# Block 2's pair entries: TensorE's product with the values issued ahead of the next entry's transposes, in one kernel of two transformer-like blocks

## The reference

```python
x = x + 0.5 * swiglu(rmsnorm(x, ffn1_norm[l]), ...)
h = rmsnorm(x, mix_norm[l])
(c_q, c_kv, k_rope, n_q, n_kc, n_vc, n_ks, n_vs, n_kw, n_vw, n_gate, sb_q, sb_k, sb_v) = jnp.split(h @ w_in[l], split_at, axis=-1)
o_mla = mla_attention(c_q, c_kv, k_rope, ...)          # 6 heads, causal
o_nsa = nsa_attention(n_q, n_kc, n_vc, n_ks, n_vs, n_kw, n_vw, gates, ...)   # 6 heads, three branches
o_sb = stick_breaking_attention(sb_q, sb_k, sb_v)      # 4 heads
x = x + concat([o_mla, o_nsa, o_sb]) @ w_out[l]
x = x + 0.5 * swiglu(rmsnorm(x, ffn2_norm[l]), ...)
```

```python
p = masked_softmax(q_block @ k.T * scale, mask)
o = p @ v
```

## Time and profile before

| | |
|---|---|
| Time, median of 3 runs | 3455.21 us (3454.33 to 3456.77) |
| Profiled execution | 3456.97 us, its span 3455.2 us |
| TensorE busy | 3352.7 us, 97% of the span |
| VectorE, ScalarE, GpSimd busy | 1668.8, 1223.1, 239.0 us |
| The two layers' stretches with pair entries | 1839.7 to 1999.0 us and 2904.0 to 3064.0 us |
| Granted TensorE clock over the execution | 0.991 of full speed |

### The profile page before, as it was taken

One profiled execution on the slowest core, in us unless ns is written; L12 is line 12 of the kernel. 1 busy time (PEld: TensorE's weight loads), 2 busy tenths in 40 slices (PEclk: granted clock), 3 DMA queues, 4 the chain that ended last, 5 costly groups with the idle time before them and its releaser, 6 DMA issues. The chain is left out here.

```text
span 3455.2 us, 42101 instructions
## 1 busy us (share of the span) xinstructions
PE 3352.7 (97%) x15684; PEld 2625.5 (76%) x15684; DVE 1668.8 (48%) x2158; ACT 1223.1 (35%) x1831; POOL 239.0 (7%) x268
## 2 busy tenths in 40 slices
PE   8999999999899999999999999999999999999998
PEld 6657888776688887888766688887888776678887
DVE  6755443566444335443545554435443554654433
ACT  4333122432422234232444442234223354542233
POOL 1200000011010000000102300002000101300000
PEclk9999999999999999999999999999999999999999
DMA  6213322321233232332321133333332321023332
GB/s 169 64 46 80 97 98 97 92 80 44 73 93 97 98 102 75 97 97 97 86 60 29 31 98 97 97 97 93 97 97 98 91 69 37 19 87 97 97 97 67
DMA packets 434262, 288.19 MB, mean 83 GB/s; under 512 B 44528, under 2 KB 412316, under 8 KB 433896
## 3 DMA queue, kind: packets, MB, share of 16 engines
q1 hardware_dynamic: 431272, 280.02, 27.9%
q0 software_dynamic: 2736, 4.58, 0.9%
q10 hardware_dynamic: 144, 2.10, 0.2%
HBM read 284.53 MB, written 2.13 MB: 83 GB/s over the span
## 5 line engine op out<-in xcount | busy, mean ns | idle before, releaser
L2018 PE MATMUL bank<-hh,whi 128*128 128x512 f32 x2768 | 1093.2, 395 | 20.3 <-DVE hl L1466 7.3
L2019 PE MATMUL bank<-hl,whi 128*128 128x512 f32 x2768 | 1079.7, 390 | 0.0
L2020 PE MATMUL bank<-hh,wlo 128*128 128x512 f32 x2768 | 1079.6, 390 | 0.0
L1400 DVE TENSOR_TENSOR wlo<-raw,whi 128x1024 fp32r<-128x1024 f32 (+2 forms) x534 | 646.4, 1212 | 309.4 <-ACT whi L944 295.0
L2018 PEld LDWEIGHTS bank<-hh,whi 128*128 128x128 f32 x2768 | 521.0, 188 | 154.9 <-issue 37.4
L944 ACT ACTIVATE whi<-raw 128x1024 fp32r<-128x1024 f32 (+2 forms) x534 | 546.4, 1034 | 258.3 <-PE bank L2020 257.8
L2020 PEld LDWEIGHTS bank<-hh,wlo 128*128 128x128 f32 x2768 | 520.8, 188 | 109.6
L2019 PEld LDWEIGHTS bank<-hl,whi 128*128 128x128 f32 x2768 | 521.1, 188 | 108.2 <-issue 2.6
L2018 PE MATMUL bank<-fshi,whi 128*128 128x512 f32 (+1 forms) x1358 | 525.6, 387 | 2.7 <-ACT G L1090 1.6
L2020 PE MATMUL bank<-fshi,wlo 128*128 128x512 f32 (+1 forms) x1358 | 521.8, 384 | 0.0
L2019 PE MATMUL bank<-fslo,whi 128*128 128x512 f32 (+1 forms) x1358 | 521.8, 384 | 0.0
(11 more groups left out here) (254 smaller groups left out, 2571.9 us busy)
## 6 DMA issues: line engine op xcount, KB each, us to landing
raw<-in_ffn_w_gate SPq DMA_DIRECT2D x88, 512.0 KB, 3.8
raw<-in_ffn_w_up SPq DMA_DIRECT2D x88, 512.0 KB, 3.8
raw<-in_ffn_w_down SPq DMA_DIRECT2D x88, 512.0 KB, 3.5
raw<-in_w_in SPq DMA_DIRECT2D x78, 512.0 KB, 3.9
raw<-in_w_up SPq DMA_DIRECT2D x64, 512.0 KB, 4.0
raw<-in_w_down SPq DMA_DIRECT2D x64, 512.0 KB, 3.4
raw<-in_w_out SPq DMA_DIRECT2D x16, 512.0 KB, 4.0
raw<-in_w_in SPq DMA_DIRECT2D x18, 256.0 KB, 3.3
```

The lines of the kernel that those rows point to most:

```text
L1400: dve.tensor_tensor(slot3(wlo, s, m), slot3(raw, s, m), slot3(whi, s, m).bitcast(F32), ALU.subtract).then_inc(c.lo_done.sem, 1)
L2018: pe.matmul(o, wh, ah, start=start, stop=False)
L2019: pe.matmul(o, wh, al, start=False, stop=False)
L2020: return pe.matmul(o, wl, ah, start=False, stop=stop)
```

## The change

In each step of `pair` TensorE now issues scores, then the product of entry j - 5, then the transposes of entry j - 4. No instruction is added or taken away, and the other engines' lists stay as they are. Lines shift in the changed kernel: the product is at L2167 (L2157 for `cmp`), the transposes at L2188 (L2183 for `cmp`).

```diff
--- before.py
+++ after.py
@@ -2142,26 +2142,6 @@
                     for head in range(2):
                         ins = pe.matmul(bank[:, sb_ + head, at:at + P], identb, causal, start=False, stop=True)
                     ins.then_inc(c.pair_qk.sem, 1)
-                k = j - T_LAG
-                if 0 <= k < n_entries:
-                    e = entries[k]
-                    if k:
-                        before = entries[k - 1]
-                        pt = c.pair_pt[before["act"]]
-                        pe.wait_ge(pt.sem, pt.at(l, before["moved"]))
-                    else:
-                        pe.wait_ge(c.cmp_sub.sem, c.cmp_sub.at(l, 1))
-                    if e["kind"] == "cmp":
-                        pe.wait_ge(c.cmp_p.sem, c.cmp_p.at(l, 1))
-                        for head in range(2):
-                            for i in range(QT):
-                                ins = pe.transpose(bank[0:32, 4 + head, P * i:P * i + P], g(C_P + 128 * (e["t"] + 3 * head) + 32 * i, 32), ident)
-                    else:
-                        pe.wait_ge(c.pair_scaled.sem, c.pair_scaled.at(l, 2 * e["q"] + 2))
-                        for head in range(2):
-                            for kt in range(e["i"] + 1):
-                                ins = pe.transpose(bank[:, 4 + head, P * kt:P * kt + P], p_tile(e, head, e["n"])[:, P * kt:P * kt + P], ident)
-                    ins.then_inc(c.pair_turned.sem, 1)
                 k = j - O_LAG
                 if 0 <= k < n_entries:
                     e = entries[k]
@@ -2187,6 +2167,26 @@
                                 ins = pe.matmul(bank[r[0]:r[1], 6, at:at + P], g(v, HD), pt_tile(e)[:, head, P * kt:P * kt + P],
                                                 start=e["first"] and kt == 0, stop=last and kt == e["i"])
                     ins.then_inc(c.pair_pv.sem, 1)
+                k = j - T_LAG
+                if 0 <= k < n_entries:
+                    e = entries[k]
+                    if k:
+                        before = entries[k - 1]
+                        pt = c.pair_pt[before["act"]]
+                        pe.wait_ge(pt.sem, pt.at(l, before["moved"]))
+                    else:
+                        pe.wait_ge(c.cmp_sub.sem, c.cmp_sub.at(l, 1))
+                    if e["kind"] == "cmp":
+                        pe.wait_ge(c.cmp_p.sem, c.cmp_p.at(l, 1))
+                        for head in range(2):
+                            for i in range(QT):
+                                ins = pe.transpose(bank[0:32, 4 + head, P * i:P * i + P], g(C_P + 128 * (e["t"] + 3 * head) + 32 * i, 32), ident)
+                    else:
+                        pe.wait_ge(c.pair_scaled.sem, c.pair_scaled.at(l, 2 * e["q"] + 2))
+                        for head in range(2):
+                            for kt in range(e["i"] + 1):
+                                ins = pe.transpose(bank[:, 4 + head, P * kt:P * kt + P], p_tile(e, head, e["n"])[:, P * kt:P * kt + P], ident)
+                    ins.then_inc(c.pair_turned.sem, 1)
 
             def compressed_scores(c, b, l):
```

## The result

The changed kernel took 3468.32 us in the median of six runs (3463.63 to 3474.04), the kernel before 3455.19 us in the six beside it (3453.40 to 3456.77). The ratio is 1.0037, with a 95% interval from 1.0027 to 1.0048: 13.1 us more, slower, and by more than the 0.2% that the prediction took as the least that can be told. The prediction was 3465.6 us in a range from 3458 to 3471, and slower. The profiled execution of the changed kernel took 3465.51 us (span 3463.7).

What follows compares the result with a forecast made beforehand. TensorE, busy 97% of the span, was taken as the bound. Delays of 4.85 us a layer, 9.7 for both, plus 0.8 for shape changes made 10.5; 3455.2 + 10.4 = 3465.6 us, range 3458 to 3471.

Steps and rivals of the forecast that it cites:

- main mechanism: Copies in pair steps have less cover; where slack is under the product's length, TensorE waits: 9.7 us for both layers.
- The reason for the sign: In pair steps VectorE's copy, not GpSimd's scaling, comes last and releases product and transposes together, so these waits gain nothing.
- First turn: From 1859.75 to the wait ending at 1874.42: late copies and late `hl` end that wait 1.05 us later a layer.
- VectorE is then busy without a break: After the late `hl`, VectorE has no idle time up to the copy awaited until 1874.42, so that wait ends 1.05 later.
- Behind `mix_lo`: In a turn's first step, transposes no longer run inside the wait for `hl` and add their length: 1.6 us a layer.
- ScalarE's copy: Transposes at 1934.70: the product in front makes ScalarE's copy end later than TensorE reaches its wait, 0.5 us a layer.
- Last step: Transposes at 1984.61: the product of 0.59 comes first, so copy start and wait end 0.6 us later a layer.
- Three like places: Near 1885, 1918 and 1952, later transposes delay the copy by 0.37, 0.31 and 0.41: 1.1 us a layer, less sure.
- Shape changes: Eight steps a layer with branch scores following get one more array shape change, 0.1 to 0.15 each: 0.4 us a layer taken.

Runs made afterwards that it cites:

- the filled kernel: Changed kernel with needless products put into three of TensorE's waits a layer; 3460.95 us, 1.0016 of the kernel before.
- only_new: Kernel before, with the product ahead of the transposes only in the six steps a layer whose product opens a turn; 3460.87 us, ratio 1.0018.
- not_new: Kernel before, with the product ahead of the transposes in all steps except the six a layer whose product opens a turn; 3463.76 us, ratio 1.0025.
- covered: Kernel before, with the product first only in 13 steps a layer (11 really change) whose next copy wait has other work ahead; 3457.97 us, ratio 1.0007.
- the second measurement: The changed kernel run once more, unaltered, beside the kernel before; 3472.08 us, ratio 1.0047.
- first_turn: Kernel before, with the product ahead of the transposes only in steps 6 to 12 of a layer; 3459.06 us, ratio 1.0012.
- the filled kernel before: Kernel before, order unchanged, with needless products put into its two waits of steps 9 and 12; 3455.19 us, ratio 0.9999.

## Why the prediction was right, and what it missed

The sign, the range and the main mechanism held; the way to the number did not, and that the forecast lies within 3 us of the result is partly luck. 10.5 us had been forecast as delay alone: 9.7 of waits and 0.8 of shape changes. The priced waits grew by 5.0 us a layer for 4.85. But the stretch grew by 3.0 to 3.2 at full clock, 6.0 to 6.5 in both layers (5.3 in the filled kernel's timed runs), since steps got shorter where I had them longer. And TensorE's clock, which the prediction took as 1.00 throughout and never named, added 2.5 a layer in the profile. Two errors of opposite sign nearly cancelled. (A slip of 0.1 besides: the sum is 10.5 and 10.4 was added.)

The terms, each as the lateness that is left behind its place:

- *The reason for the sign* held. All copy waits stand at the product and none at the transposes, and no wait for GpSimd's scaling appeared at L2188.
- *First turn, predicted 1.05.* The copy of 1864.30 did come late and `hl` was late by 1.03 (below, VectorE of the changed kernel against the earlier trace rows, each taken from the start of its stretch, which lay 0.52 earlier). But the wait behind it ended only 0.70 later: 1874.60 - 1829.89 = 44.71, against 1874.42 - 1830.41 = 44.01. The step that failed is "VectorE is then busy without a break": it was, but its work got shorter.

```profile
1867.82 0.70 DVE L1963 TENSOR_TENSOR hl<-G,hh 128x512 fp32r<-128x512 f32 x1 [0.60 <-ACT hh L1354]
...
1869.54 0.80 DVE L1628 TENSOR_TENSOR G<-G,tab 32x512 f32<-32x512 f32 x1
...
1871.56 0.68 DVE L1631 TENSOR_TENSOR G<-G 32x512 f32<-32x512 f32 x1
```

The same addition in the kernel before:

```profile
1870.92 1.15 DVE L1631 TENSOR_TENSOR G<-G 32x512 f32<-32x512 f32 x1
```

- *Behind `mix_lo`, predicted 1.6 and measured 1.04* (only_new, first layer), though the waits for `hl` grew by the full 1.6. Three of the four terms came within 0.14 of what I had reckoned (0.18 for 0.32, 0.42 for 0.47, 0.40 for 0.54). In the fourth, 0.54 less 0.27, less than 0.1 was left: what stands behind took up more of it than the 0.27 that I took off.
- *ScalarE's copy, predicted 0.5.* The wait for L1056 is 0.6 us and new. With the 0.31 of the place ahead of it, 0.81 had been forecast up to there, and the step is 0.75 later (not_new, second layer, at full clock).
- *Last step, predicted 0.6.* Its wait is 1.05 for 0.46, and the rest of the stretch ends 0.53 later.
- *Three like places, predicted 1.1.* In the second layer of not_new, from weight product to weight product, the place like that near 1885 took 0.03 us more than before (2955.84 to 2962.88 for 2951.84 to 2958.85), that like 1918 0.36 (2985.13 to 2994.85 for 2981.18 to 2990.54), and that like 1952 0.45 (3014.87 to 3024.76 for 3010.34 to 3019.78). That is 0.84 for 1.1: the first was covered by slack, and the other two came as estimated.
- *Shape changes, predicted 0.4 a layer.* This is the term that was most wrong. Measured, it is a gain of 1.2 a layer over the 11 changed steps of covered. The Trainium skill (TensorEngine Tiling (Array Packing), Key Properties) has each change of mode drain the array; here a gap disappeared where another came, and the sum of both got smaller.
- *The clock, not predicted.* A fall costs 1.5 us at the first place and 1.0 at the second, both in each layer of the changed kernel's profile: 5 us there. In the timed runs an estimate comes from the mean clock. Within one program, 0.001 less of mean clock goes with some 2 us (only_new: 3459.13 at 0.991, 3464.95 at 0.988; a straight line through the runs of the others with 11 runs gives 1.3 to 3.0), and 3.46 us would be the whole loss at a constant clock (0.001 of 3460). The changed kernel lay 0.0032 below before in the second measurement, and 0.0020 below the 0.9905 of the other groups in the first, for which I have no clock of before's own runs. That makes 4 to 7 of the 13.1, and 6 to 11 of the 16.4. This is the clock of the whole execution, so it holds more than the falls in the stretches. The changed kernel's own times, spread over 10 us in the first measurement where before's spread over 3, go with this; in the second they spread over 2.3.

The Trainium skill (TensorE: Matmul & The Clock Gate, HAM oscillation — how this bites in real kernels) says that waits between groups of products can send TensorE back to its lower clock. The rows agree in kind: the fall of 1875 came at the end of a wait of 1.99 us and isn't there in the profile with the wait filled. It also came in a stretch where TensorE is busy over 90% of the time, and in one layer of a program and not in the other.

What stays open is which waits bring a fall. The longest wait for a copy, 1.6 us before and 2.0 in the changed kernel, had one behind it in no layer of before's profile and in all four layers of the two profiles of the changed kernel; but only_new had one behind 1.60, and not_new none behind 1.97 in its second layer. covered and first_turn show falls at steps where no wait was added, and the filled kernel before has one near 2978.

## What to carry to other kernels

When a producer and its consumer share a buffer with one copy between them, issue next the work that starts the copy, and let the product whose copy is already waited for cover it; before pricing a swap, check which engine's list really starts the copy, because a delay there is only partly passed on. On an engine that is nearly always busy, price a longer wait twice: its own length, and the risk that the clock falls behind it, which in the profiles here cost nearly as much as the order itself (2.5 against 3.0 to 3.2 us a layer). A few needless products in the wait are a cheap test of that. Look in the test's profile too, since in one kernel here the fall was then at another place. And don't read the price of an order off the waits alone: here they grew by 5.0 us a layer and the stretch by 3.0 to 3.2, since transposes ahead of weight products took 0.1 us a step less than products there.

## What the hardware showed that I had not expected

TensorE's granted clock fell to 0.50 in stretches in which TensorE is busy over 90% of the time, with waits of at most 2.0 us, and did so in only one of two equal layers of the same execution (only_new, not_new). A fall cost 1.5 us at one place and 1.0 or, with a wait behind it that took up the rest, 0.35 at another. The kernel with three waits a layer filled with needless products was 11 us faster (3472.08 to 3460.95), of which its profile shows 4.7 in the stretches with the filler.

VectorE's addition at L1631, the same 32 x 512 elements, took 1.15 us before and 0.68 after. GpSimd's scaling (L921) runs beside the first (1867.49 to 1871.53) and had ended before the second (1867.32 to 1870.99). The 13 profiles hold this addition 26 times: 16 times with the scaling beside it, always 1.15, and 10 times without, always 0.68. Nothing was changed in order to vary the two apart, so that the overlap is the cause is strongly suggested and not shown; another operation on 32 x 512 elements (L1628) took only 0.70 with the scaling beside it.
